# A hybrid decoder layer on one core: where VectorE and TensorE take up expert pairs, and the order of work at the change of blocks

## The chip, the cores and the metric

The kernel runs on one core of one Trainium2 chip. The metric is the device time of one execution in microseconds, and lower is better. All data is float32.

## The reference

One decoder layer on 1024 tokens of width 1024: a mixer (sliding-window attention beside a gated delta rule), a residual and a LayerNorm, then a retrieval of single-neuron experts (PEER), a residual and a LayerNorm. Cut to what matters here:

```python
h1 = layer_norm(ALPHA * x + mix(x) @ w_out, ln1_g, ln1_b)
q = (h1 @ w_query).reshape(L, 8, 2, 128)            # L: 128 tokens
s = einsum("lhpd,hpkd->lhpk", q, sub_keys)          # 8 heads, 2 sides, 128 keys
vals, idx = top_k(s, 16)
cand = vals[..., 0, :, None] + vals[..., 1, None, :]
best, pos = top_k(cand, 16)                         # 16 of 256 for each head
expert = (idx0 * 128 + idx1)[pos]                   # 8 * 16 = 128 experts a token
u, v = expert_u[expert], expert_v[expert]           # rows of 1024 numbers each
g = gelu(einsum("ld,lhkd->lhk", h1, u)) * softmax(best)
out = layer_norm(ALPHA * h1 + einsum("lhk,lhkd->ld", g, v), ln2_g, ln2_b)
```

Each token reads 128 rows of u and 128 rows of v, so a block of 128 tokens reads 128 times 1 MB from the tables.

## The kernel before

The 1024 tokens are worked in 8 blocks of 128 tokens (block 0 to block 7). A block goes through `mix`: input projection (11 chunks of weights, 1 MB each), attention, delta rule, output projection (chunks 11 to 14), first norm, queries (chunks 15 to 22), key scores, and the choice of experts in four parts (`top`, `more`, `sel`, `rest`, `pick`, each with a number from 0 to 3). Four of the 23 chunks stay in SBUF (`kept`); the others go through two buffers (`chunk`), loaded from SP's queue when PE is done with the chunk two places before (`chunk_used`).

**Gathers.** POOL issues one indirect DMA for each of a block's 128 expert slots. Slot j brings one row of u and v for every token (1 MB) into one of 8 places of `ring`. Gather j waits until PE has used the row that lay in its place (`added`), and the first of a block wait until VectorE has written the numbers of their experts (`staged`, at the end of each `pick`).

**Pairs.** Two slots make a pair, 64 pairs a block. For a pair, VectorE makes two dot products of u with the token rows in `x_pair` (L1434), ScalarE makes GELU, gate and a diagonal matrix of it (L1007 to L1014), and PE multiplies that with v and sums in `expert_sum` (L770, 8 matmuls), which frees both places of the ring.

**The order is written out by hand.** The pairs are no loop of their own: they are set between the steps of `mix`. After each step every engine calls `mark(name)`, and the tables `EARLIER` and `OWN` say how many pairs belong to that mark. Block n's own pairs begin at `top1`, once the first quarter of its experts is staged (`OWN`, 15 pairs); the other 49 are done in the marks `rope` to `pick0` of block n + 1 (`EARLIER`). VectorE and ScalarE take the pairs of a mark up to its end; PE takes them one pair late (`b - 1`), so that it need not wait for the newest diagonal.

```python
mix(n, Marks(lambda a, b: experts(n - 1, b - 1), lambda a, b: experts(n, b - 1)), turn_over)
```

**The change of blocks** lies behind `pick0`. VectorE's `turn_over` waits for PE's last pair of the earlier block, reads the sums (`read_sums`, L1452), copies the gates (`by_pair`, L1414) and writes the four quarters of `x_pair` (`stage_rows`, L1423); then comes `top1`. PE does its last key scores (L731), the last pair and the four rows of the second norm (`ln_row`, L514), and goes on with the next block's input chunks, one ahead of each mark of `NEXT_IN` (`in_chunk`). Chunk 3 waits for the second norm of the earlier block (`out_ready`, set at L1140 behind the mark `sel1`), because both use a PSUM bank.

**Around the first norm.** PE writes the rows of the first norm (L514) between the delta rule and the mark `dn`, and waits there for `o_copied`; then for `dn_out`, transposes (L504) and multiplies the four output chunks (L485). VectorE adds the residual (L1338), makes statistics, waits for ScalarE's root (L951), scales and shifts. In block 0, which has no earlier pairs, PE fills waits with spare matmuls (`keep_busy`).

## Time and profile before

| | |
|---|---|
| time, median of 3 runs | 3286.3 us (3279.1 to 3301.65) |
| the profiled execution, its own time | 3299.78 us |
| its span in the profile | 3297.8 us |
| busy: PE, DVE (VectorE), ACT (ScalarE), POOL | 75%, 68%, 35%, 36% |
| DMA: bytes, mean rate over the span | 1254.22 MB, 380 GB/s |
| mean granted clock of TensorE | 0.867 of 2.4 GHz |

The profiled execution lies 13.5 us above the median of the three runs, inside their range. Of the page's 40 slices of 82 us, all but a few show the DMA engines at 9 tenths or more; the second and third are those of block 0, before the first gathers. The busy shares of the engines are averages over stages with different limits, so the sections below go by stretches of some microseconds.

### The profile page before, as it was taken

Reading aid. Unit: us, or ns where it says so; the run is one execution under the profiler, and the core shown is the slowest. Engines: PE = TensorE matmul, PEld = TensorE weight load, DVE = VectorE, ACT = ScalarE, POOL = GpSimd, SP = SyncE. Lnnn points to the kernel's source line nnn. Section 1 sums busy time; section 2 is a strip of 40 time slices with the busy share of each in tenths; the row PEclk is TensorE's granted clock in tenths of the full one; section 3 lists DMA queues with packets and bytes.
Section 4 is the critical chain, followed back from the end, with each engine's and each line's share of the span. In section 5 each row is a group of like instructions: output and inputs, shape, how many; then the busy total and the mean of one; then the engine's idle time right before and its main releaser. Section 6 shows DMA issues by size and latency. Waiting matters only on the chain.

```text
span 3297.8 us, 37601 instructions
## 1 busy us (share of the span) xinstructions
PE 2467.9 (75%) x11896; PEld 1386.4 (42%) x11896; DVE 2230.8 (68%) x5593; ACT 1142.6 (35%) x3499; POOL 1181.9 (36%) x1028
## 2 busy tenths in 40 slices
PE   8886778867887677967779777886788867775554
PEld 6673335524455233643346433552345523341111
DVE  3378755886568865787558875588656876579444
ACT  3213532244333533325232353233523353332222
POOL 0023442334432443334432344333433244333443
PEclk9998888888899797987989888898988969887777
DMA  8069999999999999998999999999999999989997
GB/s 329 7 265 387 415 404 411 380 394 386 409 393 410 385 417 406 371 418 361 420 386 398 391 414 403 408 385 392 414 412 383 409 368 410 417 348 352 419 420 319
DMA packets 174886, 1254.22 MB, mean 380 GB/s; under 512 B 20185, under 2 KB 20313, under 8 KB 23521
## 3 DMA queue, kind: packets, MB, share of 16 engines
q0 software_dynamic: 147456, 1073.81, 79.8%
q1 hardware_dynamic: 25056, 172.66, 12.7%
q10 hardware_dynamic: 2176, 5.36, 0.4%
q8 instruction: 95, 1.56, 0.2%
q14 instruction: 103, 0.84, 0.1%
HBM read 1247.56 MB, written 4.19 MB: 380 GB/s over the span
## 4 chain that ended last, share of the span: by engine, by line
PE 37%; DMA 29%; DVE 18%; ACT 8%; issue 5%; POOL 2%; another core or an unknown queue 0%; DVEq 0%; POOLq 0%; SPq 0%; ACTq 0%
DMA ring<-in_uv,expert_used 22%; PE expert_sum L770 14%; PE bank L493 8%; DVE ring L1434 8%; DMA chunk<-in_weights 7%; PE bank L485 6%; POOL ring L445 2%; ACT diag L1014 2%; PE bank L499 1%; PE bank L595 1%; ACT arena L874 1%; PE bank L504 1%; ACT h_raw L1007 1%; PE bank L686 1%; PE bank L685 1%
## 5 line engine op out<-in xcount | busy, mean ns | idle before, releaser
L445 POOL DMA_INDIRECT ring<-in_uv,expert_used x1024 | 1181.7, 1154 | 2086.5 <-PE expert_sum L770 1592.1
L770 PE MATMUL expert_sum<-ring,diag 128*64 128x512 f32 x4096 | 1202.4, 716 | 654.2 <-ACT diag L1014 652.3
L1434 DVE CUSTOM_DVE_ANT_0 ring<-ring,x_pair 128x1024 f32<-128x1024 f32 x1024 | 1230.9, 1223 | 599.7 <-DMA ring<-in_uv,expert_used 588.0
L770 PEld LDWEIGHTS expert_sum<-ring,diag 128*64 128x64 f32 x4096 | 311.9, 155 | 1289.8 <-issue 1275.4
L1007 ACT ACTIVATE h_raw<-h_raw 128x2 f32<-128x2 f32 x512 | 104.2, 204 | 1558.2 <-DVE h_raw L1434 1542.0
L1014 ACT ACTIVATE diag<-const,h_raw 128x64 f32<-128x64 f32 x1024 | 292.7, 332 | 0.0
L1010 ACT ACTIVATE h_raw<-h_raw,gate_used 128x1 f32<-128x1 f32 x1024 | 245.6, 286 | 16.8
L493 PE MATMUL bank<-o_cat,chunk 128*128 128x128 f32 x1376 | 173.5, 287 | 41.7 <-DMA chunk<-in_weights 41.7
L493 PEld LDWEIGHTS bank<-o_cat,chunk 128*128 128x128 f32 x1376 | 165.8, 201 | 78.2 <-DMA chunk<-in_weights 46.8
L493 PEld LDWEIGHTS bank<-oT,chunk 128*128 128x128 f32 x1344 | 152.7, 192 | 22.7 <-issue 22.7
L493 PE MATMUL bank<-oT,chunk 128*128 128x128 f32 x1344 | 158.6, 277 | 0.0
L485 PE MATMUL bank<-chunk,oT 128*128 128x256 f32 x480 | 121.2, 410 | 16.8 <-DMA chunk<-in_weights 16.8
L1157 DVE MAX8 arena<-arena 128x8 f32<-128x128 f32 (+1 forms) x384 | 103.8, 326 | 43.7 <-ACT arena L966 38.5
L499 PEld LDWEIGHTS bank<-arena 128*128 128x128 f32 x768 | 97.3, 203 | 56.8 <-issue 49.1
L485 PEld LDWEIGHTS bank<-chunk,oT 128*128 128x128 f32 x480 | 95.8, 204 | 53.9 <-DMA chunk<-in_weights 23.7
L499 PE MATMUL bank<-arena 128*128 128x128 f32 x768 | 108.9, 295 | 6.1 <-DVE arena L1273 1.6
L485 PE MATMUL bank<-chunk,o_cat 128*128 128x256 f32 x352 | 83.6, 392 | 13.7 <-DMA chunk<-in_weights 13.7
L1007 ACT ACT_TABLE_LOAD x72 | 92.4, 1283 | 1.3
L962 ACT COPY arena<-bank 128x512 f32<-128x512 f32 x32 | 18.8, 586 | 209.7 <-PE bank L493 201.1
L485 PE MATMUL bank<-kept,o_cat 128*128 128x256 f32 x256 | 81.0, 486 | 7.6 <-DMA kept<-in_weights 7.6
L1434 DVE DVE_READ_ACCUMULATOR2_ANT h_raw<- 128x1 f32 x1024 | 84.0, 82 | 0.0
L485 PEld LDWEIGHTS bank<-chunk,o_cat 128*128 128x128 f32 x352 | 66.7, 195 | 34.8 <-issue 26.2
(239 smaller groups left out, 2561.2 us busy)
## 6 DMA issues: line engine op xcount, KB each, us to landing
chunk<-in_weights SPq DMA_DIRECT2D x137, 1024.0 KB, 17.1
ring<-in_uv,expert_used POOLq DMA_INDIRECT x1024
ring<-in_weights SPq DMA_DIRECT2D x15, 1024.0 KB, 19.7
o_cat<-in_xT SPq DMA_DIRECT2D x8, 512.0 KB, 13.4
kept<-in_weights SPq DMA_DIRECT2D x4, 1024.0 KB, 14.5
x<-in_x SPq DMA_DIRECT2D x8, 512.0 KB
out<-oT ACTq DMA_DIRECT2D x8, 512.0 KB
sub_keys<-in_sub_keys ACTq DMA_DIRECT2D x1, 1024.0 KB
```

The costliest lines, as they stand in the source:

```text
L445: pool.indirect_dma_start(out=ring[:, (j % RING) * 2 * D:(j % RING + 1) * 2 * D], out_offset=None, in_=io["uv"], in_offset=bass.IndirectOf ...
L485: mm = pe.matmul(out, act[:, k, :], w[:, k, :], start=(k == 0), stop=(k == KT - 1))
L493: mm = pe.matmul(out, w[:, k, i * P:(i + 1) * P], act[:, k, :], start=(k == 0), stop=(k == KT - 1))
L499: mm = pe.matmul(out[:, hs], lhsT[:, hs], rhs[:, hs], start=True, stop=True)
L504: mm = pe.transpose(out[:, h * P:(h + 1) * P], in_[:, h * P:(h + 1) * P], ident)
L595: mm = pe.matmul(bank[4][:, h * HD:(h + 1) * HD], arena[:, A_PT * 512 + i * P:A_PT * 512 + (i + 1) * P], vrows[:, s, g * HD:(g + 1) * HD], ...
L770: mm = pe.matmul(expert_sum[i][c * SPAN:(c + 1) * SPAN, :], diag[:, (j % DIAGS) * SPAN:(j % DIAGS + 1) * SPAN], ring3[:, j % RING, D + i * ...
L1007: act.activation(h_raw[:, pair[0]:pair[1] + 1], h_raw[:, pair[0]:pair[1] + 1], ACT.Gelu).then_inc(gelued.sem, 1)
L1010: act.activation(h_raw[:, j:j + 1], h_raw[:, j:j + 1], ACT.Copy, scale=gate_used[:, j:j + 1]).then_inc(weighted.sem, 1)
L1014: act.activation(diag[:, (j % DIAGS) * SPAN:(j % DIAGS + 1) * SPAN], C["halves"], ACT.Copy, scale=h_raw[:, j:j + 1]).then_inc(diag_ready.s ...
L1157: ins = dve.max(values[:, one[part]], one[2])
L1434: dve.tensor_tensor_reduce(u, u, x_pair[:, (j % 2) * D:(j % 2 + 1) * D], 1.0, 0.0, ALU.mult, ALU.add, h_raw[:, j:j + 1]).then_inc(dotted.s ...
```

## The change

It does seven things to the order of the work; no arithmetic changes, and every pair is still computed once.

1. One pair moves from `dn` (2 before, 1 now) to a new mark `turned`, the first of `OWN` (16 pairs now). It stands right behind `turn_over`, ahead of VectorE's first half of `top1`.
2. PE is still one pair late, except at `pick3` (`PROMPT`), where it takes that mark's pair too.
3. VectorE's mark `att_o` moves ahead of its wait for PE's attention output; `out3` moves ahead of its wait for the last output chunk; `scale1` and `shift1` move one place forward each.
4. PE's rows of the first norm move from ahead of `dn` to behind the fourth output chunk, ahead of its mark `out3`; the mark `dn` moves ahead of the waits. `keep_busy` in block 0 goes from 9 to 5.
5. At the change of blocks PE does the last pair of the earlier block ahead of the last key scores, and `second_norm_rows` behind them.
6. VectorE's `turn_over` copies the gates and the two cross quarters of `x_pair` before it waits for PE, and only the two others after `read_sums`.
7. The input chunks of the next block move one mark forward on PE and ScalarE (`in_chunk(n + 1, 0)` ahead of `top1`, chunk 1 ahead of `more1`, and so on).

```diff
-    merge64=1, solve=2, ws0=1, kv0=2, ws1=1, kv1=1, dn=2, o_T=1, ...
+    merge64=1, solve=2, ws0=1, kv0=2, ws1=1, kv1=1, dn=1, o_T=1, ...
...
-OWN = {name: 1 for name in ("top1",) + NEXT_IN + AFTER_IN}
+OWN = {name: 1 for name in ("turned", "top1") + NEXT_IN + AFTER_IN}
+PROMPT = ("pick3",)
...
-            pairs(self.done, self.done + count)
+            pairs(self.done, self.done + count - (0 if name in PROMPT else self.late))
...
 # PE, mix
-                pe.wait_ge(late_in, late)
+                mark("dn")
+                pe.wait_ge(*state_new.at(n, 2))
                 pe.wait_ge(*o_copied.at(n, 2))
-                ln_row(LN1_G, 0, ln1_rows)
-                ln_row(LN1_B, 1, ln1_rows)
-                mark("dn")
-                pe.wait_ge(*state_new.at(n, 2))
                 pe.wait_ge(*dn_out.at(n, 1))
...
                     tokens_out(n, IN_CHUNKS + c, ...)
+                    if c == OUT_CHUNKS - 1:
+                        pe.wait_ge(late_in, late)
+                        ln_row(LN1_G, 0, ln1_rows)
+                        ln_row(LN1_B, 1, ln1_rows)
                     mark(f"out{c}")
...
-                keep_busy(early, 9)
+                keep_busy(early, 5)
...
                 mark("pick0")
+                turn_over(n)
                 score_keys(3)
-                turn_over(n)
+                if n > 0:
+                    second_norm_rows(n)
+                mark("turned")
+                if onward:
+                    in_chunk(n + 1, 0)
                 mark("top1")
-                for c, name in enumerate(NEXT_IN):
-                    if onward:
+                for c, name in enumerate(NEXT_IN, 1):
+                    if onward and c < IN_CHUNKS:
                         in_chunk(n + 1, c)
                     mark(name)
...
             def turn_over(n):
                 experts(n - 1, PAIRS)
-                second_norm_rows(n)
                 taken[0] = 0
...
 # ACT, mix
                 key_scores_out(3)
+                mark("turned")
                 mark("top1")
-                for c, name in enumerate(NEXT_IN):
+                for c, name in enumerate(NEXT_IN, 1):
...
 # DVE, mix
+                mark("att_o")
                 dve.wait_ge(*att_o.at(n, 1))
                 tt(o_cat[:, 0:512]...).then_inc(att_out.sem, 1)
-                mark("att_o")
                 mark("norms")
...
                     if i == 0:
                         mark("out2")
+                        mark("out3")
                 ins.then_inc(residual.sem, 1)
                 norm_stats(...)
-                mark("out3")
+                mark("scale1")
                 norm_scale(...)
-                mark("scale1")
+                mark("shift1")
                 norm_shift(...).then_inc(x1_ready.sem, 1)
-                mark("shift1")
                 mark("x1_T")
...
-            def stage_rows(n):
-                by_pair(gate_used, gate, 0, PART)
-                dve.wait_ge(*sums_read.at(n, 0))
+            def stage_rows(n, own):
                 for s in range(2):
-                    for c in range(2):
-                        ins = dve.tensor_copy(x_pair[s * SPAN:(s + 1) * SPAN, c * D:(c + 1) * D], x1[c * SPAN:(c + 1) * SPAN, :])
-                ins.then_inc(rows_staged.sem, 1)
+                    c = s if own else 1 - s
+                    ins = dve.tensor_copy(x_pair[s * SPAN:(s + 1) * SPAN, c * D:(c + 1) * D], x1[c * SPAN:(c + 1) * SPAN, :])
+                return ins
...
             def turn_over(n):
-                dve.wait_ge(*chunk_used.at(n, CHUNKS))
-                read_sums(n - 1)
-                stage_rows(n)
+                if n > 0:
+                    dve.wait_ge(*added.at(n - 1, 2 * PART))
+                by_pair(gate_used, gate, 0, PART)
+                stage_rows(n, False)
+                if n > 0:
+                    dve.wait_ge(*chunk_used.at(n, CHUNKS))
+                    read_sums(n - 1)
+                stage_rows(n, True).then_inc(rows_staged.sem, 1)
```

## Rows read from the trace of the kernel before

**Rows 1.** The page, its line on the DMA packets of the whole execution.

```profile
DMA packets 174886, 1254.22 MB, mean 380 GB/s; under 512 B 20185, under 2 KB 20313, under 8 KB 23521
```

**Rows 2.** Windows: length, PE, PEld, DVE, ACT, POOL busy (count), PEclk, DMA share, GB/s.

```profile
68.00:195.00 127.00, 111.84 (x633) 85.70 (x633) 52.62 (x156) 34.11 (x59) 2.14 (x3) 0.92 0.03 9
1580.00:1600.00 20.00, 15.27 (x95) 9.28 (x94) 12.78 (x22) 7.01 (x25) 9.46 (x8) 1.00 1.02 421
1884.00:1890.00 6.00, 6.00 (x24) 1.69 (x20) 5.93 (x20) 3.13 (x12) 1.83 (x2) 0.77 0.31 90
1535.00:1542.00 7.00, 6.23 (x15) 1.33 (x12) 6.37 (x12) 3.99 (x13) 3.50 (x2) 0.50 0.27 78
1716.00:1720.00 4.00, 4.00 (x27) 2.45 (x26) 1.97 (x4) 2.71 (x10) 3.32 (x3) 0.98 0.62 190
1760.00:1766.00 6.00, 6.00 (x45) 4.40 (x43) 5.43 (x16) 2.66 (x6) 2.06 (x2) 1.00 0.41 139
1397.00:1404.00 7.00, 7.00 (x38) 4.92 (x39) 6.82 (x15) 1.54 (x6) 2.88 (x2) 1.00 0.82 296
2957.00:2981.00 24.00, 8.37 (x28) 1.99 (x24) 23.00 (x61) 5.12 (x18) 7.92 (x8) 0.78 0.77 288
```

**Rows 3.** Timeline, pick3 of block 4 onwards: start, length, work, [idle before].

```profile
1875.23 1.22 DVE L1434 CUSTOM_DVE_ANT_0 ring<-ring,x_pair 128x1024 f32<-128x1024 f32 x1
...
1876.42 0.94 POOL L445 DMA_INDIRECT ring<-in_uv,expert_used  x1 [0.30 <-issue]
...
1883.49 7.00 PE L770 MATMUL expert_sum<-ring,diag 128*64 128x512 f32 x24
...
1887.87 0.97 POOL L445 DMA_INDIRECT ring<-in_uv,expert_used  x1 [10.50 <-PE expert_sum L770]
...
1905.92 2.78 POOL L445 DMA_INDIRECT ring<-in_uv,expert_used  x1 [6.17 <-PE expert_sum L770]
```

**Rows 4.** Timeline, all engines, attention of block 4.

```profile
1533.71 3.68 PE L770 MATMUL expert_sum<-ring,diag 128*64 128x512 f32 x8
...
1538.19 1.69 POOL L445 DMA_INDIRECT ring<-in_uv,expert_used  x1 [8.48 <-PE expert_sum L770]
```

**Rows 5.** Waits of the whole span: total us, times, longest us.

```profile
DVE o_cat L1243 <- PE bank L595: 48.1, 8, 9.9
...
DVE small L1110 <- ACT small L951: 32.5, 8, 4.4
```

**Rows 6.** Timeline, PE, delta rule to first norm, block 4.

```profile
1653.06 3.69 PE L514 MATMUL bank<-k_keys,const 8*128 8x512 f32 x8
...
1664.45 3.68 PE L770 MATMUL expert_sum<-ring,diag 128*64 128x512 f32 x8 [5.83 <-ACT diag L1014]
...
1711.12 3.68 PE L770 MATMUL expert_sum<-ring,diag 128*64 128x512 f32 x8 [7.29 <-ACT diag L1014]
```

**Rows 7.** Timeline, all engines, change of blocks, 3 to 4.

```profile
1755.73 7.41 PE L493 MATMUL bank<-oT,chunk 128*128 128x128 f32 x64
...
1755.79 1.23 DVE L1434 CUSTOM_DVE_ANT_0 ring<-ring,x_pair 128x1024 f32<-128x1024 f32 x1 [2.85 <-DMA ring<-in_uv,expert_used]
...
1763.25 0.80 SPq L419 DMA_DIRECT2D chunk<-in_weights  x2
...
1763.64 1.17 POOL L445 DMA_INDIRECT ring<-in_uv,expert_used  x1 [15.80 <-DVE expert_used L1414]
...
1768.61 2.78 DVE L1452 SCALAR_TENSOR_TENSOR oT<-x_pair,expert_sum 64x512 f32<-64x512 f32 x4 [2.94 <-PE expert_sum L770]
...
1772.28 2.79 DVE L1423 COPY x_pair<-x 64x1024 f32<-64x1024 f32 x4
...
1772.57 1.22 POOL L445 DMA_INDIRECT ring<-in_uv,expert_used  x1 [0.30 <-issue]
```

**Rows 8.** Timeline, second norm of the earlier block, VectorE.

```profile
1795.53 1.28 DVE L1140 TENSOR_TENSOR oT<-oT,bank 128x512 f32<-128x512 f32 x2
```

**Rows 9.** Waits of VectorE, from 1775 to 1870 us.

```profile
DVE ring L1434 <- DMA ring<-in_uv,expert_used: 10.0, 6, 3.1
```

More of the change, by code:

```diff
@@ L105, with __init__ @@
 AFTER_IN = ("sel3", "rest3", "pick3")
-OWN = {name: 1 for name in ("top1",) + NEXT_IN + AFTER_IN}
+OWN = {name: 1 for name in ("turned", "top1") + NEXT_IN + AFTER_IN}
+PROMPT = ("pick3",)
 assert sum(EARLIER.values()) + sum(OWN.values()) == PAIRS and 2 * sum(OWN.values()) <= PART
 class Marks:
-    def __init__(self, earlier=None, own=None, behind={}):
+    def __init__(self, earlier=None, own=None, behind={}, late=0):
         self.names, self.behind = list(EARLIER) + list(OWN), behind
-        self.earlier, self.own, self.done = earlier, own, sum(OWN.values())
+        self.earlier, self.own, self.late, self.done = earlier, own, late, sum(OWN.values())
     def __call__(self, name):
         assert self.names.pop(0) == name
-        if name == "top1":
+        if name == "turned":
             self.done = 0
@@ L775, in experts @@
                                 mm.then_inc(added.sem, 1)
-                taken[0] = last
+                taken[0] = max(taken[0], last)
             def second_norm_rows(n):
@@ L1396, in mix @@
                         turn_over(n)
+                        mark("turned")
                 weights_out(n, 2, slice(2, PH))
@@ L1454, in read_sums @@
                 ins.then_inc(sums_read.sem, 1)
+                dve.wait_ge(*sums_read.at(n, 1))
             def second_stats(n):
@@ L1480, in marks @@
                               "sel1": lambda: second_shift(n - 1)})
-            mix(0, Marks(own=lambda a, b: experts(0, a, b)), stage_rows)
+            mix(0, Marks(own=lambda a, b: experts(0, a, b)), turn_over)
             assert steps[0] == DVE_STEPS, steps
```

11 lines of the change are left out of this document (5 added, 6 removed).

## The prediction

> **What bounds the kernel now.** I read the page's slices first, then windows of a few microseconds where the slices dip, then the timelines of the engines around each dip. The bytes alone set a floor: 1254.22 MB [rows 1] at the 421 GB/s of a full stretch (1580 to 1600) [rows 2] are 2979 us of the 3297.8 us span. The window from 68 to 195 moves 9 GB/s [rows 2]: block 0 has no pairs yet, so 124 us are idle there. The change touches that chain only by `keep_busy` and by the norm rows, both of which lie in waits. The first microseconds and the tail behind the last gather take some 35 us more. About 160 us are left, spread over blocks 1 to 7 as holes of 2 to 7 us. So the kernel is bound by its DMAs, and an edit is worth what it takes out of the holes. I cost a hole as its length times (1 - rate / 421). Because time can only be gained there, shorter waits of VectorE or PE elsewhere are worth nothing.
>
> A second rule decides how much of a hole is gained. Between one wait of VectorE for a gather and the next, the chain of the engines sets the pace, and the idle time of the DMAs in that stretch is its length less the work issued in it. If a gather is only issued earlier and the next issue is held by the chain as before, the hole moves to there. It is gained when the DMAs stay busy until VectorE waits for data again.
>
> **`pick3` taken promptly (edit 2).** VectorE's last dot product of the `pick3` pair starts at 1875.23, PE takes it up only at 1883.49, behind the next block's first transposes, and POOL stands idle for 10.50 us until 1887.87 [rows 3]. The 6 us from 1884 move 90 GB/s, so 4.7 us are lost [rows 2]. Promptly, PE would end that pair near 1881, even with TensorE's granted clock at the lower of its two levels, where a pair takes 3.68 us ([rows 4], in a window with a PEclk of 0.50 [rows 2]), and the hole closes. But the gather of 1905.92 is held by PE as before [rows 3]. I put the backlog at that moment at about 5 us, from eight gathers of 2.5 us (1.05 MB at 421 GB/s) issued since 1887.87. Some 2 us of the hole come back there, and 2.5 of 4.7 us are gained. The hole lies at all seven `rope` marks; I take this one for each. In blocks 2, 4 and 7 it is gained nowhere: PE ran at the lower clock at attention, POOL waited 8.48 us for PE until 1538.19 [rows 4], and the window from 1535 moves 78 GB/s [rows 2], so the DMAs run dry again and the hole only moves. 4 x 2.5 = **10 us**, bounds 0 and 7 x 4.7 = 33.
>
> **`att_o` ahead of the wait (edit 3).** VectorE waits there 48.1 us in all, up to 9.9 us [rows 5], and two pairs of 2.4 us (twice 1.22 [rows 3]) fit in. PE's order keeps the ring, though: the gather of 1538.19 follows the pair that PE begins at 1533.71 behind its attention matmuls [rows 4], and that one is dotted before the wait in both kernels. Cost and gain are **0**, bounds -3 and +5 us over all blocks; the copy to `o_cat` comes up to two pairs later and its reader on PE comes after the norms.
>
> **`dn`, the norm rows, out-projection and first norm (edits 1, 3, 4).** One pair less in `dn` lets PE transpose at once: now it waits for the diagonal at 1664.45 and spends 3.68 us on the pair [rows 6]. The norm rows cost 3.69 us at 1653.06, in front of a wait [rows 6]. Moved behind the fourth chunk, they run beside VectorE's residual and statistics, and hold back one free ring place by 3.7 us. ScalarE's root, for which VectorE waits 32.5 us in all [rows 5], is late because ScalarE first serves the `out3` pair that VectorE dots between statistics and scale. That pair now lies in front of the last output chunk, so the root comes some 4 us earlier. The chain to `x1_ready` gains 4 us by this and PE is no longer held by the pair of 1711.12 (7.29 us of waiting and 3.68 us of work [rows 6]). That pair's late release makes the hole of 1716 to 1720 (190 GB/s, 2.2 us [rows 2]). Five blocks have one of about that size, 11 us in all. Behind it VectorE waits for data, so what closes is gained: **9 us**, bounds 4 and 11. The hole behind the `dn` chain stays, since VectorE's chain there is the same.
>
> **Change of blocks (edits 1, 5, 6, 7).** From 1755.73 PE does the last query chunks [rows 7]. Only when they are used, at 1763.25, can SP issue the next two chunks of weights, 2 MB or 5 us of DMA work; POOL's first gather of the block is issued at 1763.64, when the experts are staged. Both come too late: 1760 to 1766 moves 139 GB/s, 4.0 us lost [rows 2]. VectorE waited for a gather until 1755.79, and the choice of experts behind it takes the same time as before, so the staging isn't sooner. But PE starts the queries some 5 us earlier and should end them about 3 us before the staging; then the weights fill part of the hole. I take 1.7 us in each of six blocks, **10 us**, bounds 0 and 6 x 4.0 = 24. The last block has no next weights and keeps its hole.
>
> `turn_over` has 2.3 us of copies less behind the wait that ends at 1768.61 (0.89 us for the gates, between 1768.61 + 2.78 and 1772.28, and half of 2.79 for the rows [rows 7]). In their place VectorE dots the `turned` pair, 2.4 us. Its second gather lands near 1775 (two of 2.5 us and two weight chunks behind an issue at 1763.64), so VectorE waits 2 us there. PE waits one key-score copy more, and reaches input chunk 3 one mark sooner, while `out_ready` comes only behind 1795.53 + 1.28 [rows 8]: 2 to 4 us of waiting, with the next pair's release where it was. What hides both is that VectorE waits 10.0 us for gathers before this part ends [rows 9]. In return the first places of the ring come free 1 to 3 us sooner. The hole of 1397 to 1404 (296 GB/s, 2.1 us [rows 2]) stands in four blocks: **4 us**, bounds 0 and 8. In the last block nothing but pairs feeds the DMAs; 2957 to 2981 moves 288 GB/s, 7.6 us lost [rows 2], and as much again until VectorE waits for data. One pair (2 x 2.5 us) in hand there takes **5 us**, bounds 2 and 8.
>
> The copies that move ahead of the wait run beside POOL's first gather issues. The trace has such neighbours: the issue at 1772.57, beside the copy of 1772.28, took 1.22 us instead of 0.94 [rows 3, 7], 0.28 us, below anything counted here. The Trainium skill, page SBUF — State Buffer, section "SBUF: two separate sides", says more: an fp32 `tensor_copy` within SBUF locks GpSimd out, so that it cannot write descriptors and the DMA stands still for the whole copy. By that rule the first gathers would wait for all 2.3 us of copies, and the sum would be 16 us less.
>
> **The sum.** 10 + 0 + 9 + 10 + 4 + 5 = 38 us. Against the profiled execution 3299.8 - 38 = 3261.8 us, a ratio of 0.9885; on the median of 3286.3 us, which is 13.5 us lower, that is **3248 us**.
>
> **Rivals.** *The holes only move* (second rule, everywhere): the `rope` and weights terms go to nothing and the norm term to half, and 4 + 4 + 5 = 13 us are left, two more if a `rope` hole closes: 15 us, 3271 us. For it speaks that three of seven blocks already show the second hole. *More closes than I take*: the weights fill the change of blocks (24 us) and the `rope` holes close in most blocks (25 us with 9 + 4 + 5), 67 us, 3220 us. For it speaks that edit 3 also frees ScalarE earlier before the norms. *Slower, by the `turned` pair*: VectorE's 2 us, PE's key-score copy of 2 us and its 4 us for `out_ready` come to 8 us a block. They decide once they exceed the 10.0 us of cover [rows 9]. If that cover has gone, because the holes before it closed, all 8 count in seven blocks, and only 9 + 5 + 8 = 22 us are gained: 56 - 22 = 34 us slower, 3320 us. Against it speaks that the added pair itself asks 5 us more of the DMAs in that part, so that the cover grows. *POOL is locked out* by the moved copies: 2.3 x 7 = 16 us of the 38 gone, 3264 us; one row says 0.28 us instead.
>
> **From there to the numbers.** Forecast 0.45, holes move 0.26, more closes 0.12, slower 0.11, lock 0.06. A measurement of this kernel can tell about 1% from no change, 33 us; the forecast lies 5 us beyond, so its share is split 0.28 faster to 0.17 same. Faster 0.28 + 0.12 = 0.40 (plus 0.02 from the tail of holes moving), same 0.47, slower 0.11. The range leaves out the slower rival's far half and the bounds' far end: 3212 to 3300.
>
> **What the profile would show.** PE's `pick3` pair ends ahead of the transposes and POOL's idle time there falls from 10.50 to about 5 us. The wait for ScalarE's root falls from 32.5 us to below 10, that for attention from 48.1 to below 30. SP issues two weight chunks ahead of POOL's first gather of a block. The mean rate rises from 380 to 385 GB/s. It would be wrong if the `turned` pair's wait for data is followed by no wait near the end of that part, or if the lower clock falls on attention in more blocks than three.

## The result, and the profile after

The changed kernel takes 3300.3 us (median of 20 runs, 3286.39 to 3319.23) against 3286.66 us for the kernel before (20 runs): a ratio of 1.004, 95% interval 1.0027 to 1.0053. It is slower by some 14 us. The forecast was 38 us faster. The profiled execution took 3303.56 us, with a span of 3301.6 us and a granted clock of 0.867, as before.

The page's line on the DMA packets shows the same bytes at the same mean rate as in [rows 1]; the forecast was 385 GB/s.

```profile
DMA packets 174885, 1254.22 MB, mean 380 GB/s; under 512 B 20184, under 2 KB 20312, under 8 KB 23520
```

VectorE's waits in the changed kernel, as in [rows 5] and beside them the wait for gathers:

```profile
DVE ring L1440 <- DMA ring<-in_uv,expert_used: 699.3, 489, 5.4
...
DVE small L1117 <- ACT small L957: 1.9, 1, 1.9
...
DVE o_cat L1251 <- PE bank L596: 1.7, 3, 1.0
```

The wait for attention fell from 48.1 to 1.7 us and the one for ScalarE's root from 32.5 to 1.9 us. VectorE's wait for gathers stood at 588.0 us before and is 699.3 us now, 111 us more: what the edits saved on the engines was waited for again as data.

Windows of the changed kernel at the places of [rows 2], with its own times; columns as there:

```profile
1760.00:1766.00 6.00, 4.64 (x16) 1.89 (x16) 3.50 (x11) 1.16 (x5) 4.78 (x5) 0.56 0.96 337
2960.00:2985.00 25.00, 11.70 (x32) 2.68 (x28) 23.82 (x70) 7.06 (x20) 8.24 (x9) 0.64 0.89 358
1886.00:1890.00 4.00, 3.94 (x10) 1.38 (x12) 4.00 (x15) 2.20 (x8) 0.00 (x0) 0.50 0.92 387
1890.00:1893.00 3.00, 3.00 (x11) 1.11 (x8) 1.97 (x4) 0.96 (x5) 2.05 (x2) 0.74 0.35 79
```

The hole at the change of blocks has mostly gone (139 to 337 GB/s) and the one of the last block has halved (288 to 358 GB/s). A new one stands at 1890 to 1893: 79 GB/s over 3 us, 2.4 us lost, behind four microseconds of TensorE at a PEclk of 0.50. This is how it comes about, in the timeline from `pick3` of block 4 onwards (it answers to [rows 3]):

```profile
1875.03 1.22 DVE L1440 CUSTOM_DVE_ANT_0 ring<-ring,x_pair 128x1024 f32<-128x1024 f32 x1
...
1877.63 3.68 PE L777 MATMUL expert_sum<-ring,diag 128*64 128x512 f32 x8 [5.51 <-ACT diag L1021]
...
1881.24 1.09 PE L556 MATMUL bank<-const,arena 128*64 128x128 f32 x8
...
1882.09 0.93 POOL L446 DMA_INDIRECT ring<-in_uv,expert_used  x1 [6.17 <-PE expert_sum L777]
...
1886.06 6.37 PE L777 MATMUL expert_sum<-ring,diag 128*64 128x512 f32 x16 [3.52 <-ACT diag L1021]
...
1890.52 1.11 POOL L446 DMA_INDIRECT ring<-in_uv,expert_used  x1 [6.26 <-PE expert_sum L777]
...
1892.36 3.72 PE L569 MATMUL bank<-k_keys,arena 64*128 64x256 f32 x16
...
1893.53 0.69 DVE L1225 SCALAR_TENSOR_TENSOR arena<-bank,const 128x512 f32<-128x512 f32 x1 [1.55 <-PE bank L569]
```

PE does the `pick3` pair 5.66 us sooner behind its dots than before (1877.63 behind 1875.03, against 1883.49 behind 1875.23), and POOL's idle time falls from 10.50 to 6.17 us. But then PE stands idle for 3.52 us, and the next two pairs take 6.37 us, where two at the full clock take 3.9 (1.94 each). POOL waits 6.26 us again, PE reaches the attention scores later, and now VectorE waits for them.

This place is one of the worse ones. Over blocks 1 to 7 the attention scores on PE start 9.3 to 11.7 us behind VectorE's first `rope` dot, on average 10.6, where it was 9.1 before. VectorE's wait for them is 0.2 to 1.8 us in six of the seven blocks, 6 us in all. In the kernel before it does not wait there in any block.

Where it ends up in a block can be read from the starts of VectorE's dot products, as means over the pairs of blocks 1 to 6, in us (worked out from the traces; "block" is `pick0` to `pick0`). Each row is one execution. Those of `before` and `gates_wait_moved` took 13 us more than the median of their kernel, that of `prompt_only` 8 us more, the others at most 5: differences of 1 to 2 us a block that involve these three rows say little.

```
                           rope to  rope to  rope to  pick0 to
                            scores    decay    pick0      rope   block
before                        16.4     62.3    271.4     121.2   392.6
prompt_only                   16.3     62.1    271.8     121.0   392.8
after                         18.0     63.2    268.1     124.0   392.1
after_no_prompt               16.6     60.4    265.5     123.7   389.2
three_spare                   16.6     61.2    265.1     124.4   389.5
gates_wait_moved              16.3     61.7    266.6     124.8   391.4
```

### The profile page after: what moved, and what is told of

Its sections match the earlier page's. It is cut to its first block, busy times and chain, and to the rows that moved or that the text cites. A ratio compares the mean times of both kernels' runs of the same rounds, so it can differ in the third digit from the quotient of the medians.

```text
span 3301.6 us, 37592 instructions
## 1 busy us (share of the span) xinstructions
PE 2488.3 (75%) x11888; PEld 1385.3 (42%) x11888; DVE 2234.5 (68%) x5593; ACT 1146.7 (35%) x3499; POOL 1143.3 (35%) x1028
## 4 chain that ended last, share of the span: by engine, by line
DMA 33%; PE 31%; DVE 20%; ACT 7%; issue 6%; POOL 2%; DVEq 0%; SPq 0%; POOLq 0%; ACTq 0%
DMA ring<-in_uv,expert_used 26%; PE expert_sum L777 12%; DVE ring L1440 9%; PE bank L494 7%; DMA chunk<-in_weights 6%; PE bank L486 4%; POOL ring L446 2%; ACT diag L1021 2%; PE bank L500 1%; PE bank L596 1%; ACT arena L880 1%; DVE arena L1164 1%; PE bank L569 1%; PE bank L515 1%; ACT L1014 1%
## 5 line engine op out<-in xcount | busy, mean ns | idle before, releaser
L446 POOL DMA_INDIRECT ring<-in_uv,expert_used x1024 | 1143.1, 1116 | 2127.8 <-PE expert_sum L777 1617.1
L777 PE MATMUL expert_sum<-ring,diag 128*64 128x512 f32 x4096 | 1228.5, 732 | 648.4 <-ACT diag L1021 648.0
L1440 DVE CUSTOM_DVE_ANT_0 ring<-ring,x_pair 128x1024 f32<-128x1024 f32 x1024 | 1233.6, 1223 | 703.9 <-DMA ring<-in_uv,expert_used 699.3
L777 PEld LDWEIGHTS expert_sum<-ring,diag 128*64 128x64 f32 x4096 | 322.5, 159 | 1311.3 <-issue 1297.4
L1014 ACT ACT_TABLE_LOAD x72 | 92.4, 1283 | 22.5 <-DVE h_raw L1440 21.3
L486 PE MATMUL bank<-kept,o_cat 128*128 128x256 f32 x256 | 74.3, 454 | 8.1 <-DMA kept<-in_weights 8.1
L515 PE MATMUL bank<-k_keys,const 8*128 8x512 f32 x128 | 74.9, 734 | 4.7 <-ACT arena L972 4.7
```

The costliest lines, as they stand in the source:

```text
L446: pool.indirect_dma_start(out=ring[:, (j % RING) * 2 * D:(j % RING + 1) * 2 * D], out_offset=None, in_=io["uv"], in_offset=bass.IndirectOf ...
L486: mm = pe.matmul(out, act[:, k, :], w[:, k, :], start=(k == 0), stop=(k == KT - 1))
L515: mm = pe.matmul(banks[i][:, :], ident[LN_ROWS, k:k + 1].to_broadcast([8, P]), k_keys[LN_ROWS, :], start=True, stop=True)
L777: mm = pe.matmul(expert_sum[i][c * SPAN:(c + 1) * SPAN, :], diag[:, (j % DIAGS) * SPAN:(j % DIAGS + 1) * SPAN], ring3[:, j % RING, D + i * ...
L1014: act.activation(h_raw[:, pair[0]:pair[1] + 1], h_raw[:, pair[0]:pair[1] + 1], ACT.Gelu).then_inc(gelued.sem, 1)
L1440: dve.tensor_tensor_reduce(u, u, x_pair[:, (j % 2) * D:(j % 2 + 1) * D], 1.0, 0.0, ALU.mult, ALU.add, h_raw[:, j:j + 1]).then_inc(dotted.s ...
```

## The experiments

Ratios are to the kernel before, each in five rounds, with the 95% interval. [rows n] and the numbers of the edits are those of the sections above.

### One group of edits at a time

Four kernels put one group on the kernel before: `prompt_only` edit 2, `att_only` the `att_o` part of edit 3, `norm_only` edit 4 and the rest of edit 3, `change_only` edits 1, 5, 6 and 7.

```diff
 # att_only, DVE                      # prompt_only
+                mark("att_o")        +PROMPT = ("pick3",)
                 dve.wait_ge(*att_o.at(n, 1))
                 tt(o_cat ...)
-                mark("att_o")
 # norm_only, PE
-                ln_row(LN1_G, 0, ln1_rows)     # ahead of dn
...
+                    if c == OUT_CHUNKS - 1:
+                        ln_row(LN1_G, 0, ln1_rows)
```

> The kernel before with PE taking the pick3 pair promptly (edit 2) and nothing else. Forecast: 10 us faster, ratio 0.997. Theory A: within 0.2%, the hole at rope gone and one of the same size behind the scores pairs or at attention in its place. If the prompt pair holds PE's transposes of the next block back, 3 to 7 us slower.

Measured: 1.0026 (1.0008 to 1.0045), 3298.93 us.

> The kernel before with VectorE's mark att_o ahead of its wait for PE's attention output and nothing else. Theory A and the forecast: no change, within 0.2%. If two pairs in front of the wait hold VectorE for gathers that have not landed, so that the attention output and the norms come late, it is 5 us or more slower.

Measured: 0.9996 (0.9974 to 1.0019), 3283.41 us.

> The kernel before with the marks out3, scale1 and shift1 moved forward and PE's rows of the first norm behind the fourth output chunk (edit 4 and half of edit 3), dn still with 2 pairs. Theory A: within 0.2% of before. Forecast: 9 us faster, ratio 0.997. If the norm rows, now ahead of the out3 pair on PE, hold back a place of the ring that the gathers need (theory C), it is 5 to 15 us slower, ratio 1.002 to 1.005, with a hole behind out3.

Measured: 0.9975 (0.9958 to 0.9991), 3279.37 us.

> The kernel before with the new change of blocks alone (edits 1, 5, 6, 7), the rest as before. If the holes of the DMAs only move (theory A), the time stays within 0.2% of before. If the parts of my forecast hold, it is 19 us faster (10 at the change, 4 behind it, 5 in the last block), ratio 0.994. If the new slow part sits here, because VectorE waits for the second gather of the turned pair and PE for out_ready (theory B), it is 10 us or more slower, ratio 1.003 or above.

Measured: 0.9995 (0.9974 to 1.0015), 3287.48 us.

The norm group is worth what was forecast, attention nothing, as forecast; the change of blocks is worth next to nothing and the prompt pair costs. The product of the four is 0.9992. The whole is 1.004, so the parts also seem to hurt each other, by about 0.5%; with four intervals in the product this is only just clear of chance, and the next group of runs has it more sharply.

### The change without one group

```diff
 # after_no_prompt
-PROMPT = ("pick3",)
+PROMPT = ()
```

`after_no_att` and `after_no_norm` take the edits of `att_only` and `norm_only` back, `after_no_change` is edits 2, 3 and 4 on the kernel before.

> The changed kernel with PE one pair late at pick3 again (edit 2 undone). Alone, edit 2 was 0.26% slower. Theory D (the prompt pair costs by itself, in the last block because the rows of the second norm then stand ahead of the next pairs, elsewhere because its hole only moves): ratio to before falls from 1.004 to about 1.001. Theory E (the parts hinder each other, whichever): some other undoing matters more, and this one stays at 1.003 or above.

Measured: 0.9969 (0.9952 to 0.9986), 3278.51 us.

> The changed kernel with VectorE's mark att_o behind its wait again. Alone, that edit was level. Theory E1: with one pair more at each point of the chain, the att_o pairs have not landed (VectorE waits 4.9 us for them in a block of the changed kernel), so in front of the wait they hold attention's output and the norms back: undone, the ratio falls by 0.002 or more to about 1.002. Theory D: no change, 1.004.

Measured: 1.0029 (1.0007 to 1.005).

> The changed kernel with edit 4 and the marks out3, scale1 and shift1 as before. Alone, that edit was 0.25% faster. If it also gains in company, undoing it gives 1.006. Theory E2 (with dn at one pair and the norm rows behind the fourth chunk, PE frees no place for 4 us where the ring is dry): undoing it gives 1.002 or below.

Measured: 1.0037 (1.0011 to 1.0062).

> The kernel before with edits 2, 3 and 4, the change of blocks as before (dn with 2 pairs, no turned pair). The parts alone sum to 0.9997 (0.9975, 1.0026, 0.9996). If the parts only add, 1.000. If the interaction lies with the shifted pair (theories E1 and E2), this one is at 1.000 or below while the others stay above; if it lies among edits 2, 3 and 4 themselves, this one is near 1.004.

Measured: 1.0015 (0.9995 to 1.0035).

Only one of them stands out, and by more than any expectation had it (1.001). Without the prompt pair the change is faster than the kernel before; with it, it loses 0.7% (1.004 to 0.9969), 23 us, where it costs 0.26% alone; the difference of 0.45% is clear of the intervals (0.3% together). PE in `after_no_prompt` at the same place:

```profile
1870.12 1.89 PE L556 MATMUL bank<-const,arena 128*64 128x128 f32 x8 [8.49 <-DVE arena L1208]
1871.79 0.64 PE L559 MATMUL bank<-const,arena 128*64 128x128 f32 x2
1872.36 7.33 PE L777 MATMUL expert_sum<-ring,diag 128*64 128x512 f32 x24
1879.62 3.72 PE L569 MATMUL bank<-k_keys,arena 64*128 64x256 f32 x16
```

Three pairs run without a gap. The first pays for the lower clock; the `gates` pair, the last ahead of attention, is at the full one (a PEclk of 0.87 over 1875 to 1880). From VectorE's first `rope` dot (1870.02 here, 1880.94 in the changed kernel) to the attention scores on PE it is 9.60 us here and 11.42 us there, for the same work (9.3 and 10.6 us as means over blocks 1 to 7), and VectorE never waits for the scores here.

### Is it the last block?

In `prompt_only` PE takes the four rows of the second norm in the last block (7.19 us) ahead of the next pairs, where the kernel before does pairs, so the last block was a suspect. PE in `prompt_only`:

```profile
3041.07 3.68 PE L771 MATMUL expert_sum<-ring,diag 128*64 128x512 f32 x8 [4.47 <-ACT diag L1015]
3044.68 7.19 PE L515 MATMUL bank<-k_keys,const 8*128 8x512 f32 x8
3051.80 9.78 PE L771 MATMUL expert_sum<-ring,diag 128*64 128x512 f32 x32
```

```diff
-            mix(NB - 1, Marks(..., late=1), turn_over, onward=False)
+            mix(NB - 1, Marks(..., late=1, prompt=()), turn_over, onward=False)
```

> The changed kernel, with pick3's pair taken promptly by PE in blocks 0 to 6 and one pair late in block 7 as everywhere else. Taking it promptly costs the changed kernel 0.7% (from 0.9969 to 1.004 of the kernel before). Theory A, last block: PE reaches the four rows of the second norm sooner and they stand in front of the next pairs; nothing but pairs feeds the DMAs there. If that is all of the cost, the ratio is 0.997. Theory B, every block: behind the prompt pair PE idles before the rope pair, its granted clock falls and attention starts 1.4 us later in each of seven blocks. If that is all, the ratio stays at 1.004. The holes of block 7 (some 5 us against under 1 us) let me expect mostly B: 1.0025 to 1.003.

Measured: 1.005 (1.0025 to 1.0074), where 1.0025 to 1.003 was expected. The last block is not the place for the changed kernel. For `prompt_only` it may be one, which no run tried: its blocks are about as long as those of before (392.8 against 392.6 us), and its DMAs lose 6.9 us in this window, where the kernel before moves 360 GB/s at the same place (3040 to 3053) and loses 1.9 us:

```profile
3046.00:3059.00 13.00, 13.00 (x29) 3.98 (x30) 4.74 (x8) 3.69 (x15) 3.55 (x5) 0.57 0.57 197
```

### The engines' chain by itself

Gathers of half the size (the row of u alone; v is not loaded and PE multiplies what lies in the ring) bring the bytes down to 717 MB and the mean rate to 242 to 248 GB/s. The bandwidth of the DMAs is no bound any more, and what is timed is the chain of the engines, with the issue and the landing of a gather in it: VectorE still waits 109 to 159 us for gathers.

```diff
-  out=ring[:, (j % RING) * 2 * D:(j % RING + 1) * 2 * D], out_offset=None, in_=io["uv"],
+  out=ring[:, (j % RING) * 2 * D:(j % RING) * 2 * D + D], out_offset=None, in_=io["uv"],
```

> The changed kernel with gathers of half the size: of each expert only the row of u is loaded, and PE multiplies what lies in the ring in place of v, so the output is not the reference's. The bytes fall to some 740 MB and the DMAs are no bound, so the time is that of the engines' chain. I expect 0.85 to 0.92 of the kernel before. Beside the same kernel without the prompt pair: if the chain is what the prompt pair makes longer (1.4 us in each of seven blocks and up to 5 us in the last), this one is 8 to 15 us slower. If the chain is the same and the loss is one of when gathers are issued, the two are equal within 3 us.

Measured: 2923.35 us (2913.59 to 2926.12).

> The same with half gathers (rows of u alone, output not the reference's) and with pick3's pair one pair late on PE. By the chain theory 8 to 15 us faster than the changed kernel with half gathers; by the theory that only the moment of issue counts, equal within 3 us.

Measured: 2903.56 us (2896.55 to 2907.01).

> The kernel before with half gathers (rows of u alone, output not the reference's): how long its engines' chain is. If the five other parts of the change shorten the chain (norm rows and first norm some 4 us a block), it takes 2904 + 7 x 3 to 4 = 2925 to 2932 us. If their 0.3% came from the DMAs' order alone, it takes 2904 us, as the changed kernel without the prompt pair.

Measured: 2981.99 us (2971.99 to 2983.69).

Two things follow. The prompt pair makes the chain 20 us longer, with the DMAs far from full; in the traces VectorE's wait for gathers grows from 137.4 to 159.2 us. And the rest of the change makes the chain 78 us shorter, where 21 to 28 were expected, and of which the full kernel shows 10 (0.9969). Most of the 78 us lie between `rope` and `pick0`, 244 us a block before and 233 with the change, while `pick0` to `rope` is 114 us in both, one pair more or not. Time saved on the chain was mostly given back to the wait for data; time lost at `rope` was not covered by it.

### The clock, or the order?

Spare matmuls behind the first transposes of blocks 1 to 7 fill PE's 3.5 us of idle time in the changed kernel. First twelve:

```diff
                 mm.then_inc(att_T.sem, 1)
+                if not early:
+                    for _ in range(12):
+                        pe.matmul(bank[2][64:128, :], ident[:, 0:64], const[:, 0:512], start=True, stop=True, tile_position=(0, 64))
                 mark("rope")
```

> The changed kernel, with 12 spare matmuls of a pair's form (128x64 by 512 columns, results unused) on PE behind the first transposes of each block but the first, where PE now stands idle 3.5 us and its granted clock falls to 0.5. 12 of them are 2.9 us at the full clock, 5.5 us at half. If the lower clock is what makes the prompt pair dear, the rope and gates pairs take 1.94 us each and the ratio falls from 1.004 to about 0.999. If it is not the clock but the order (the prompt pair ahead of the transposes, the chain of attention behind it), the ratio stays at 1.004, or rises to 1.006 where the spare matmuls end after the diagonal of the rope pair is ready.

Measured: 1.0108 (1.0081 to 1.0136). The price was wrong: they took over 9 us, not 2.9, and held the `rope` pair until 1519.88, 10 us behind its second dot. (A spare matmul shows as two records; the first row has 21 of the 24.)

```profile
1511.23 9.23 PE L563 MATMUL bank<-const 128*64 128x512 f32 x21
1519.88 0.64 PE L780 MATMUL expert_sum<-ring,diag 128*64 128x512 f32 x1
```

The run shows another thing: some 6 us of delay at this place in seven blocks cost 22 us against the changed kernel (1.0108 to 1.004), about half of it coming through to the end. Then three, with nothing else changed:

> The changed kernel (prompt pair kept, 1.004) with three spare matmuls in place of twelve behind the first transposes of blocks 1 to 7. Twelve took 9.2 us and held the rope pair 5 us; three are 2.6 us and fit into the 3.5 us for which PE stands idle there. Clock theory: rope and gates pairs fall from 6.4 to 3.9 us together, attention starts as early as without the prompt pair or earlier, and the ratio comes to 0.997 to 1.000. Order theory: 1.004 as before.

Measured: 0.9982 (0.9962 to 1.0002), 3283.82 us.

> The changed kernel with half gathers (rows of u alone, output not the reference's) and with the same three spare matmuls; without them 2923 us, and 2904 us without the prompt pair. Clock theory: 2900 to 2910 us. Order theory: 2923 us.

Measured: 2907.74 us (2902.19 to 2911.26), against 2923.35 without the three.

```profile
1878.18 2.79 PE L563 MATMUL bank<-const 128*64 128x512 f32 x6
1880.94 1.94 PE L780 MATMUL expert_sum<-ring,diag 128*64 128x512 f32 x8
1883.25 1.94 PE L780 MATMUL expert_sum<-ring,diag 128*64 128x512 f32 x8 [0.38 <-ACT diag L1024]
1885.12 3.72 PE L572 MATMUL bank<-k_keys,arena 64*128 64x256 f32 x16
```

The order of the work is that of the changed kernel, more is done, and 0.6% is won back: both pairs take 1.94 us, in all seven blocks. The scores start 9.3 us behind the first `rope` dot, as without the prompt pair, and VectorE's wait for them is gone. So it is TensorE's clock through which the prompt pair costs most of its price in the changed kernel, and the clock is down because of the idle time behind it. Block 4 of the changed kernel says the same: there both pairs ran at the full clock (1.94 us each) in the order of the change, and the scores started 9.3 us behind the dot. What the runs don't show is the whole way to the 19 to 23 us: the scores come 1.3 us later on average, which is 9 us in seven blocks, and the rest arises behind them. The other attempt was to lift the clock in `after_no_prompt`, with five matmuls of `keep_busy`'s form in front of the wait for the rotated heads:

```diff
+                if not early:
+                    for _ in range(5):
+                        pe.matmul(bank[1][:, :], ident, const[:, 0:512], start=True, stop=True)
                 pe.wait_ge(*roped.at(n, 2))
```

> The changed kernel with pick3's pair one pair late (0.9969 of before), and with five spare matmuls of 128x128 by 512 columns on PE in front of its wait for VectorE's rotated heads in blocks 1 to 7, where it stands idle 8.5 us and then works at a granted clock of 0.50. By the spare matmuls of the run before, one takes 0.88 us at the full clock, so five are 4.4 to 7 us and fit. Clock theory: the transposes fall from 2.2 to about 1.2 us and the three pairs from 7.3 to 5.9 us, attention starts 2.4 us sooner in each of seven blocks, some 15 us: 0.992 to 0.994. Order theory (the clock at this place costs nothing, the prompt pair costs by its place alone): 0.997 as without the spare matmuls.

Measured: 0.9966 (0.9947 to 0.9985), no more than without. Two rows say why:

```profile
1869.74 1.89 PE L559 MATMUL bank<-const,arena 128*64 128x128 f32 x8 [5.13 <-DVE arena L1211]
...
1877.04 1.94 PE L780 MATMUL expert_sum<-ring,diag 128*64 128x512 f32 x8 [0.37 <-ACT diag L1024]
```

The five ended 5.13 us early and the clock was down again at the transposes (1.89 us, as without them); and the last pair waited 0.37 us for ScalarE's diagonal. From the first `rope` dot to the scores it is 9.3 us here and 9.60 in `after_no_prompt` at this place, so a faster PE had 0.3 us to gain there and not the 2.4 that were expected.

### Why the diagonal comes late

This leaves the question why PE idles 3.52 us in the changed kernel and 1.14 us in `prompt_only`, although VectorE's steps are the same. PE in `prompt_only`:

```profile
1877.38 1.92 PE L556 MATMUL bank<-const,arena 128*64 128x128 f32 x8
1879.08 0.63 PE L559 MATMUL bank<-const,arena 128*64 128x128 f32 x2
1880.86 1.94 PE L771 MATMUL expert_sum<-ring,diag 128*64 128x512 f32 x8 [1.14 <-ACT diag L1015]
```

ScalarE's timeline in `prompt_only`:

```profile
1876.55 0.20 ACT L858 ACTIVATE small<-small 128x4 f32<-128x4 f32 x1
1876.77 1.28 ACT L1008 ACT_TABLE_LOAD   x1
1879.52 0.20 ACT L1008 ACTIVATE h_raw<-h_raw 128x2 f32<-128x2 f32 x1 [1.47 <-DVE h_raw L1435]
```

and in the changed kernel:

```profile
1880.41 0.20 ACT L863 ACTIVATE small<-small 128x4 f32<-128x4 f32 x1
1883.43 1.28 ACT L1014 ACT_TABLE_LOAD   x1 [2.81 <-DVE h_raw L1440]
1884.72 0.20 ACT L1014 ACTIVATE h_raw<-h_raw 128x2 f32<-128x2 f32 x1
```

The table for GELU is loaded ahead of the wait for the dots in one and behind it in the other. With 15 own pairs the `rope` pair is the 16th of its block, the last one in the first quarter of its slots; with `turned` it is the 17th, the first beyond that quarter, and the code waits there for `late_gates` too, the gates of the other three quarters. (The expectation below calls it the first of the second half.) With two waits in front of the instruction the load lies behind them, and the diagonal is 1.3 us late. It is so in each of the seven `rope` steps of all twenty traces: ahead of the dots with one wait, behind them with two. (The Trainium skill, page ScalarE: Activation LUTs, section "What ACT_TABLE_LOAD costs", gives 1283 ns for the load, as the rows show, and about 1380 ns of drain beside it; here the load starts 0.02 us behind the ACTIVATE before it (`prompt_only`) and the next ACTIVATE 0.01 us behind the load (the changed kernel), so no drain is seen.) The test takes the second wait away from there:

```diff
 # ACT, mix
+                if n > 0:
+                    act.wait_ge(*late_gates.at(n - 1, 1))
                 act.wait_ge(*gate_pre.at(n, 1))
 # ACT, experts
-                    if pair[0] == PART:
+                    if pair[0] == PART and n == NB - 1:
                         act.wait_ge(*late_gates.at(n, 1))
```

> The changed kernel, prompt pair and all, with one wait of ScalarE moved: with 16 own pairs in place of 15 the rope pair is the first of a block's second half, and ScalarE waits for the late gates in front of it (long there) beside its wait for the dot products. In every trace with the turned pair ScalarE then loads its table for GELU behind the dots (1.28 us) and the rope diagonal comes 4.0 us after them; without it the load lies ahead of the wait and the diagonal comes after 2.6 us. Here the wait for the late gates stands at the start of the block's mix, except for the last block. Theory A: this is why the prompt pair costs 0.7% in company and 0.26% alone. Then the rope pair starts 2.6 us after the dots, PE idles about 1.1 us in place of 3.5, its clock stays at 1.00 for the gates pair, attention starts 1.4 us sooner, and the ratio is 0.997 to 0.9985, as with three spare matmuls. Theory B: the table load is not what counts, the ratio stays at 1.004.

Measured: 1.0 (0.9974 to 1.0027), 3284.29 us. ScalarE in it:

```profile
1879.80 1.28 ACT L862 ACT_TABLE_LOAD   x1 [0.94 <-DVE small L1198]
...
1882.93 1.28 ACT L1015 ACT_TABLE_LOAD   x1
...
1884.76 0.20 ACT L1015 ACTIVATE h_raw<-h_raw 128x2 f32<-128x2 f32 x1 [0.54 <-DVE h_raw L1441]
```

The load at the dots is ahead of the wait again, and PE starts the `rope` pair 2.6 us behind the dots in place of 4.0. (The load of the `mix` step, which has two waits now, went behind its wait: the same rule, seen from the other side, at a place with cover.) It is so in all seven blocks, the scores start 8.9 us behind the first `rope` dot, and VectorE does not wait for them. But PE still idles 1.4 to 2.4 us, where 1.1 was expected, and in blocks 3 and 5 the `rope` pair ran at the lower clock (3.4 and 3.6 us), in the other five at the full one. 0.4% of the 0.7% is back, less than was expected, and the result lies within what the four groups give one by one (0.9992). What is left of the prompt pair's price, 1.0 against 0.9969, is about its price alone (0.26%). Whether the moved wait would also gain without the prompt pair was not tried.

### A version that beats both

Behind the output chunks the same question can be asked: what stands on PE ahead of a pair? Edit 4 put the rows of the first norm there. In `after_no_prompt`:

```profile
1679.04 4.52 PE L515 MATMUL bank<-k_keys,const 8*128 8x512 f32 x8
...
1683.48 7.90 PE L777 MATMUL expert_sum<-ring,diag 128*64 128x512 f32 x24
...
1687.96 0.94 POOL L446 DMA_INDIRECT ring<-in_uv,expert_used  x1 [9.52 <-PE expert_sum L777]
```

The pair that was dotted at 1664.9 frees its places only at 1687; POOL idles 9.52 us and the window from 1685 to 1692 moves 301 GB/s.

```diff
-PROMPT = ("pick3",)
+PROMPT = ()
...
                     tokens_out(n, IN_CHUNKS + c, ...)
+                    mark(f"out{c}")
                     if c == OUT_CHUNKS - 1:
                         pe.wait_ge(late_in, late)
                         ln_row(LN1_G, 0, ln1_rows)
                         ln_row(LN1_B, 1, ln1_rows)
-                    mark(f"out{c}")
```

> A version meant to beat both kernels: the changed kernel with pick3's pair one pair late (0.9969), and PE's rows of the first norm behind the mark out3 in place of ahead of it. With half gathers the chain behind the output chunks has PE's out3 pair end 3 us later than it could, because the rows (3.7 us at half clock) stand in front of it. If what bounds there is the release of the ring's places, as at attention, 1 to 3 us a block are gained: 0.992 to 0.995. If VectorE then waits for the rows before its scale (the rows end later by one pair, 2 to 3.7 us), as much is lost and the ratio is 0.997 to 0.999.

Measured: 0.9917 (0.9893 to 0.9941), 3261.99 us, 27 us faster than the kernel before and, by the ratios, 40 us faster than the changed one. The step from `after_no_prompt` is 0.5%, 17 us, give or take 10.

```profile
1680.63 1.94 PE L777 MATMUL expert_sum<-ring,diag 128*64 128x512 f32 x8
...
1682.49 3.69 PE L515 MATMUL bank<-k_keys,const 8*128 8x512 f32 x8
1683.37 1.63 POOL L446 DMA_INDIRECT ring<-in_uv,expert_used  x1 [3.33 <-PE expert_sum L777]
```

## Why the prediction was wrong

The first paragraph's view held: the kernel is bound by its DMAs, and gains on the engines elsewhere return as waits for data. The two half-size kernels show it more sharply than it was put (78 us of chain for 10 us of time). What failed is a step within it.

**The step that failed is "`pick3` taken promptly"**, with its bounds "0 and 7 x 4.7 = 33". It looked at the hole in front of the pair and not at what PE does behind it, and gave no reason for excluding a loss. Its first half was right: the pair ends at 1881.3, even at the lower clock, and POOL's idle time falls to 6.17 us (about 5 was said). Its sum had the gather of 1905.92 "held by PE as before". It is not: PE has no work between the transposes and the `rope` pair, idles, and runs the next two pairs mostly at the lower clock, 6.37 us for 3.9; over the seven blocks VectorE waits 6 us for scores that it never waited for before. The text had the 3.68 us pair in hand ([rows 4], PEclk 0.50) and used it for the pair that moves, not for those that stay. In place of 10 us gained the runs show 9 us lost alone (0.26%) and 23 us lost in company (0.7%). One of the signs that the prediction set itself did show: the `turn_p` pair of attention took 2.9 to 3.7 us in four blocks, three before. The clearer one stood at `rope`, where it did not look: below the full clock in six of seven blocks, none before.

**A wait that was not in the sum** joins it: the `turned` pair makes `rope` the 17th pair of its block, with a second wait on ScalarE and the table load behind it. Nothing hides 1.3 us there once PE has no pair in hand. Without the prompt pair it is hidden behind PE's own work. That is the interaction between edits 1 and 2, as far as the runs show it: moving the one wait gives back 0.4%.

**`att_o`**: 0 was forecast and 0.9996 measured; the wait fell to 1.7 us, as "below 30" had it, and was worth nothing.

**Norm**: 9 us forecast, 8 us measured (0.9975, interval 3 to 14 us), in a kernel that keeps both `dn` pairs, where the forecast had one less. But within it the rows behind the fourth chunk were said to "hold back one free ring place by 3.7 us" at no cost. Moved behind the pair they gave 17 us more (0.9969 to 0.9917), so this was the dearest thing costed at nothing. The mechanism of the term (VectorE's chain to `x1_ready`) was right; what stands in front of a pair on PE was the larger part.

**Change of blocks**: the weights term was right for the whole change. SP issues two chunks of weights 0.8 to 4.1 us ahead of POOL's first gather in blocks 1 to 6, and the six holes from `rest0` to the next block's first pair sum to 19 us, 27 before (worked out from the traces as in the prediction, in bins of 1 us with the DMA share under 0.9): 8 us for the forecast 10. But it takes the norm group too, by which PE starts the queries sooner. In `change_only` and in `after_no_norm`, which lack it, SP issues the weights from 2.3 us ahead to 0.4 us behind the first gather, and the six holes sum to 26 us in both; in `norm_only` they sum to 23. At the change from block 3 to block 4, in the changed kernel and in `change_only`:

```profile
1754.34 1.02 SPq L420 DMA_DIRECT2D chunk<-in_weights  x2
...
1758.48 1.16 POOL L446 DMA_INDIRECT ring<-in_uv,expert_used  x1 [21.62 <-DVE expert_used L1422]
```

```profile
1759.02 0.80 SPq L420 DMA_DIRECT2D chunk<-in_weights  x2
...
1759.20 1.17 POOL L446 DMA_INDIRECT ring<-in_uv,expert_used  x1 [15.79 <-DVE expert_used L1421]
```

POOL isn't locked out by the copies that moved (the rival with 0.06, and the rule of the Trainium skill, page SBUF — State Buffer, section "SBUF: two separate sides", quoted there): two issues beside VectorE's copies took 1.08 us each, 0.14 more than one alone (0.94 [rows 3]), not longer by the copies' length.

```profile
1761.19 1.08 POOL L446 DMA_INDIRECT ring<-in_uv,expert_used  x1 [0.30 <-issue]
...
1761.45 1.39 DVE L1429 COPY x_pair<-x 64x1024 f32<-64x1024 f32 x2
1762.57 1.08 POOL L446 DMA_INDIRECT ring<-in_uv,expert_used  x1 [0.30 <-issue]
...
1765.16 2.78 DVE L1458 SCALAR_TENSOR_TENSOR oT<-x_pair,expert_sum 64x512 f32<-64x512 f32 x4 [2.32 <-PE expert_sum L777]
...
1769.40 1.23 DVE L1440 CUSTOM_DVE_ANT_0 ring<-ring,x_pair 128x1024 f32<-128x1024 f32 x1
```

The `turned` pair is dotted at 1769.40 without a wait for data, where 2 us were said, so the rival that ended slower had the sign of the result and not its mechanism. `change_only` gives 0.9995, 2 us with an interval from 9 us faster to 5 slower, where 10 + 4 + 5 = 19 were forecast. The 10 could not come in that kernel, as the rows show. Of the 9 that are left the interval doesn't say much. In its trace `pick0` to `rope` is 3 us a block longer than before (124.0 us), for the pair that moved there, `rope` to `pick0` 4 to 5 us shorter (266.9 us), and the DMAs lose 34 us in the stretches from `o_T` to `more0`, where it was 21 before: the rival by which holes only move fits it best.

**What stays open.** Summed over all bins of 1 us behind 195 us in which the DMAs' share is under 0.9, they lose 152 us in the kernel before, 150 in the changed one, 132 in `after_no_prompt` and 118 in `no_prompt_rows`. Of the 26 us between the profiled executions of the changed kernel and `after_no_prompt`, 17 are thus holes, and they lie between `rope` and `decay` (57 against 40 us; the table has 2.8 us a block there), where the ring's places are freed last; from `after_no_prompt` to `no_prompt_rows` 12 us of holes go between `o_T` and `more0` (25 to 13 us). These sums are of one execution each: between kernels that are alike at `rope` they differ by up to 14 us, and the changed kernel and the one before, which differ by 2 us in holes and 4 in their spans, can't be told apart by them. Why 19 to 23 us come of 9 us of later scores is not shown. One thing stands beside it in the traces: the pair behind `softmax`, in attention, ran below the full clock in all seven blocks of the changed kernel, of `three_spare` and of `gates_wait_moved`, in two of `after_no_prompt` and in three of the kernel before. And the 0.3% between `gates_wait_moved` and `after_no_prompt` has no cause: the scores come sooner there in every block (8.9 us against 9.3), the two at the lower clock included, and the intervals overlap.

## What to carry to other kernels

Before a pair, a tile or any filler is taken out of the place where it stands, ask what the engine does in the gap that it leaves: work that looks late may be the cover for a slow producer and what holds TensorE's clock. Where DMAs are the bound, look on each engine for what stands ahead of the instruction that frees a buffer, and move that behind it; shorter waits of the engines elsewhere were worth next to nothing here. And when a count changes, follow every constant that divides the sequence, since a step can become the first of another part and inherit its wait.

## What the runs showed of the hardware

- A table load of ScalarE (1.28 us) starts ahead of its instruction's wait when there is one wait (1876.77, dots ready at 1879.5) and behind it when there are two (1883.43 and, in `gates_wait_moved`, 1879.80). It held in each `rope` step of all twenty traces. More than two waits, or other instructions, were not looked at.
- TensorE's granted clock was 0.50 for a pair behind 3.5 us of idle time and 1.00 behind 1.1 us: one pair takes 3.68 or 1.94 us. The idle time alone does not decide it: the `rope` pair took 1.94 us behind 3.73 us of it (the changed kernel, block 4) and 3.63 us behind 2.17 us (`prompt_only`, block 2). Three spare matmuls in the gap (2.79 us) kept it up; five that ended 5.13 us ahead did not.
- A spare matmul from `const` by `ident` shows as two records of 0.44 us at a PEclk of 1.00 (21 of the 24 records of 12 matmuls took 9.23 us), where one of a pair's, with the same 128x64 by 512 columns, takes 0.24 us.
